# Two transformer-like blocks on one core: the projections beside the scan as pairs of 2x2 block products, and the scan's input and results kept in DRAM

## The reference

```python
h = rmsnorm(x, norm_pre)
proj = h @ w_in
xbc, dt_raw, z_ssd, sc_h, sc_b, sc_c, z_sc = jnp.split(proj, idx, axis=-1)
xbc = silu(causal_dwconv(xbc, ssd_conv_w, ssd_conv_b))      # 10 tiles of 128
y_ssd = ssd_chunked(xs, dt, a, bm, cm, d_skip)              # the scan, 8 chunks of 128 tokens
yz = y_ssd * silu(z_ssd);  y_ssd = rmsnorm(yz)              # 8 tiles
v = causal_dwconv(sc_c * sc_h, sc_conv_w)                   # 8 + 8 tiles
y_sc = sc_b * v * silu(z_sc)                                # 8 + 8 tiles
x = x + rmsnorm(concat(y_ssd, y_sc) @ w_out, norm_post)     # then a gate; then block two
```

## Time and profile before

| | |
|---|---|
| runs | 2523.59, 2518.59, 2519.59 us |
| median | 2519.59 us |
| profiled execution | 2521.91 us |
| its span, first to last instruction | 2520.2 us |
| mean granted TensorE clock | 0.986 |
| DMA queues, mean over the span | 97 GB/s |

### The profile page before, as it was taken

One profiled execution on the slowest core, in us unless ns is written; L12 is line 12 of the kernel. 1 busy time (PEld: TensorE's weight loads), 2 busy tenths in 40 slices (PEclk: granted clock), 3 DMA queues, 4 the chain that ended last, 5 costly groups with the idle time before them and its releaser, 6 DMA issues.

```text
span 2520.2 us, 34207 instructions
## 1 busy us (share of the span) xinstructions
PE 2424.8 (96%) x12962; PEld 1985.4 (79%) x12962; DVE 1479.8 (59%) x1930; ACT 738.6 (29%) x946; POOL 1053.4 (42%) x561
## 2 busy tenths in 40 slices
PE   7999999999999899999999999999989999899995
PEld 5777888887888678777878787788877888788885
DVE  6766556556621462113156766745788666777788
ACT  4332232222200221242022222222264333343443
POOL 4433333334443554233223223233464555466661
PEclk9999999999999999999999999999999999999998
DMA  5122122213111332122222222222224444843321
GB/s 203 42 68 75 58 87 72 75 62 113 34 50 50 100 101 77 42 98 85 75 80 77 78 63 83 70 87 84 66 102 150 151 168 142 312 185 139 123 101 67
DMA packets 100937, 245.62 MB, mean 97 GB/s; under 512 B 10850, under 2 KB 36706, under 8 KB 96243
## 3 DMA queue, kind: packets, MB, share of 16 engines
q1 hardware_dynamic: 59904, 186.67, 22.2%
q10 hardware_dynamic: 40946, 57.78, 6.7%
HBM read 183.53 MB, written 60.88 MB: 97 GB/s over the span
## 4 chain that ended last, share of the span: by engine, by line
PE 80%; DVE 10%; issue 4%; ACT 2%; DMA 2%; POOL 2%; ACTq 0%; DVEq 0%; SPq 0%; POOLq 0%
PE pt L2020 47%; PE pt L2413 14%; PE wk L2413 6%; PE pt L2036 1%; PE pt L2050 1%; DMA eb<-o_d 1%; PE wk L2319 1%; PE wk L2424 1%; PE wk L2175 1%; PE wk L2289 1%; PE wk L2354 1%; DVE eb L1684 1%; PE wk L2353 1%; PE wk L2075 1%; PE wk L2176 1%
## 5 line engine op out<-in xcount | busy, mean ns | idle before, releaser
L545 POOL TENSOR_TENSOR w_hi<-w_raw,ones 128x1024 fp32r<-128x1024 f32 x138 | 269.4, 1953 | 1109.5 <-PE pt L2020 1056.5
L549 POOL TENSOR_TENSOR w_lo<-w_raw,w_hi 128x1024 fp32r<-128x1024 f32 x138 | 381.8, 2766 | 10.9
L2020 PE MATMUL pt<-xh,w_hi 128*128 128x512 f32 x960 | 300.3, 394 | 2.4 <-ACT ea L791 2.4
L2020 PE MATMUL pt<-xh,w_lo 128*128 128x512 f32 x960 | 296.6, 390 | 0.0
L2020 PE MATMUL pt<-h,w_hi 128*128 128x512 f32 x896 | 290.9, 406 | 1.8 <-ACT cu_o L903 1.8
L2020 PE MATMUL pt<-l,w_hi 128*128 128x512 f32 x896 | 278.0, 391 | 0.0
L2020 PE MATMUL pt<-h,w_lo 128*128 128x512 f32 x896 | 277.2, 391 | 0.0
L2020 PE MATMUL pt<-xl,w_hi 128*128 128x512 f32 x848 | 263.0, 391 | 0.0
L2020 PEld LDWEIGHTS pt<-xh,w_hi 128*128 128x128 f32 x960 | 179.5, 189 | 47.0 <-issue 9.4
L2020 PEld LDWEIGHTS pt<-xh,w_lo 128*128 128x128 f32 x960 | 181.0, 189 | 38.1
L2020 PEld LDWEIGHTS pt<-l,w_hi 128*128 128x128 f32 x896 | 168.8, 188 | 36.6
(11 more groups left out here) (520 smaller groups left out, 5066.5 us busy)
## 6 DMA issues: line engine op xcount, KB each, us to landing
w_raw<-ws_d SPq DMA_DIRECT2D x140, 512.0 KB, 3.6
fx_d<-stg SPq DMA_DIRECT2D x106, 256.0 KB, 2.6
fraw<-ws_d SPq DMA_DIRECT2D x32, 512.0 KB, 5.0
raw<-ws_d SPq DMA_DIRECT2D x32, 512.0 KB, 8.3
xs0f<-fx_d SPq DMA_DIRECT2D x10, 1024.0 KB, 4.8
xs1f<-fx_d SPq DMA_DIRECT2D x9, 1024.0 KB, 4.9
xs2f<-fx_d SPq DMA_DIRECT2D x9, 1024.0 KB, 5.0
x_raw<-xT_d SPq DMA_DIRECT2D x32, 256.0 KB, 7.2
```

What stands on the lines that cost most here:

```text
L545: nc.gpsimd.tensor_tensor(out=w_hi[:, u, :], in0=w_raw[:, u, :], in1=zeros, op=ALU.add).then_inc(w_hi_done, 1)
L549: nc.gpsimd.tensor_tensor(out=w_lo[:, u, :], in0=w_raw[:, u, :], in1=w_hi[:, u, :].bitcast(f32), op=ALU.subtract).then_inc(w_split, 1)
L2020: ins = MM(pt[:, slot, h * HALF:(h + 1) * HALF], wt[:, k * P:(k + 1) * P], x[:, k, h * HALF:(h + 1) * HALF], start=first and k == 0 and n ...
```

## The change

The 32 tiles beside the scan become 16 pairs. A pair's weights are four blocks of 512 inputs by 128 outputs, x is four blocks of 512 features by 512 tokens, and the pair's result (2 x 128 features by 2 x 512 tokens) is made of seven block products in place of eight, each 4 row blocks x 3 matmuls. The products need sums of weight blocks (two on DVE, two on POOL per pair) and differences of x blocks, which replace x in `x_raw` once (16 subtractions on DVE, high halves `thi` by ACT, low halves `tlo` by POOL, between the first and second convolution pair). `tlo` takes the place of `xbc`, `thi` that of `vbuf`. So the scan's input goes to DRAM (`xbc_d`) and each chunk is loaded from there by SP; the chunk's result goes to `ys_d`, the branch to `sv_d`, and both are loaded again after the scan. One block of x, `xh` and `xl` rows 0 to 3 of the second token half, isn't needed beside the scan: it is stored in `x12_d`, its place holds the ring of four weight slots, and it is loaded again for the tiles `S_SB`.

```diff
+SC_PAIRS = 2 * C
+SC_ORDER = (1, 6, 7, 5, 4, 2, 3)
@@ SyncE
+        weights(1, 4, 0)
+        sp.wait_ge(stat_done, 2)
+        sc_load(0)
...
+        for j in range(C):
+            n = 2 * j
+            if j < C - 1:
+                sp.wait_ge(sw_lo, 7 * n + 7)
+                sc_load(n + 2)
+            sp.wait_ge(y_evac, j + 1)
+            sp.dma_start(ys_d.rearrange("i p t -> p i t")[:, :, j * P:(j + 1) * P], yb[:]).then_inc(ys_put, 16)
+            if j < C - 1:
+                chunk_load(j + 1)
...
+        for n, x in enumerate((xh, xl)):
+            sp.dma_start(x[:, 0:4, cols(1)].bitcast(f32), x12_d[n, :, :, :]).then_inc(x12_in, 16)
...
+        for i in range(5, KT):
+            y_load(i)
+            v_load(i - 3)
@@ GpSimd
-        for u in range(2):
-            split(u, 16)
-            rest(u, u + 1)
+        split(0, 16)
+        rest(0, 1)
+        rest(1, 2)
...
+        for j in range(1, S_SB // 2):
+            for u in range(2):
+                pool.wait_ge(mm_done, j * 2 + u - 1)
+                split(u, j * 16 + 16)
+                rest(u, j * 2 + u + 1)
+            if j > 1:
+                for i in range(4 * j - 8, 4 * j - 4):
+                    difference_lo(i)
...
+        for g in range(SC_PRODUCTS):
+            n, i = divmod(g, 7)
+            sc_lo(g)
+            if i == 5:
+                fourth_sum(n)
+                if n < SC_PAIRS - 1:
+                    third_sum(n + 1)
@@ ScalarE
         xbc_pair(0)
...
+        for i in range(16):
+            r, c = difference(i)
+            act.wait_ge(xt_done, i + 1)
+            A(thi[:, r, c], x_raw[:, r, c], ACT.Copy).then_inc(xth_done, 1)
         xbc_pair(1)
...
+            A(sc_slot(g)[0], sc_factor(n, p), ACT.Copy).then_inc(sw_hi, 1)
...
+            tanh(j, 1)
+            if not last:
+                sc_hi(b + 8)
+                if j:
+                    decay_rows(j + 1, 0, 8)
+            sc_11(2 * j + 1)
+            tanh(j, 2)
+            if not last:
+                sc_hi(b + 9)
+                if j:
+                    decay_rows(j + 1, 8, HEADS)
...
+            tanh(j, 3)
...
         def branch_high(i):
-            act.wait_ge(mm_done, S_SB + i + 1)
+            act.wait_ge(mm_done, S_SB + max(i + 1, 2))
@@ VectorE
         conv_pair(0)
+        for k in range(4):
+            for m in range(4):
...
+                if m:
+                    dve.wait_ge(xt_done, 4 * k + m)
+                TT(out=x_raw[:, r, c], in0=x, in1=y, op=ALU.subtract).then_inc(xt_done, 1)
         conv_pair(1)
...
+        def part_x(n):
...
+            TT(out=sx5[:], in0=bank(3), in1=su2[:], op=ALU.add).then_inc(sc_part, 1)
...
+        for j in range(C):
+            a, b = 2 * j, 2 * j + 1
+            part_u2(a)
+            weight_sums(b)
+            if j > 1:
+                scan_input(j)
+            part_x(a)
+            if j > 1:
+                scan_decayed(j)
+            part_22(a)
...
+            tap(j, 1)
+            part_u2(b)
+            tap(j, 2)
+            if j < C - 1:
+                weight_sums(b + 1)
+            if j == 0:
+                scan_matrix(j)
+            elif j > 1:
+                scan_out(j)
+            part_x(b)
+            if j == 1:
+                scan_out(j)
+            if j:
+                scan_state(j)
+            part_22(b)
+            if j:
+                gate_z(j, 1)
+            part_21(b)
...
+            gate_z(j, 0)
...
+            gate_branch(j, 0)
...
+            part_12(b)
+            gate_branch(j, 1)
@@ TensorE
-        pe.wait_ge(p_lo_done, 2)
...
-            for k in range(2):
-                for m, (wt, x) in enumerate(((w_hi, p_hi), (w_hi, p_lo), (w_lo, p_hi))):
+            for m, (wt, x) in enumerate(((w_hi, p_hi), (w_lo, p_hi), (w_hi, p_lo))):
...
+        def sc_product(g):
...
+            out = bank((0, 1, 3, 2, 3, 0, 2)[i])
+            pe.wait_ge(sw_lo, g + 1)
...
+            elif i == 0:
+                pe.wait_ge(sc_t1, 2 * n)
+                if n > 1:
+                    pe.wait_ge(sc_th, (n // 2 - 1) * 4 + 3)
+            elif i < 4:
+                pe.wait_ge(sc_part, 5 * (n - 1) + (1, 4, 5)[i - 1])
+            elif i == 5:
+                pe.wait_ge(sc_t1, 2 * n + 1)
+            else:
+                pe.wait_ge(sc_part, 5 * n + (2 if i == 4 else 3))
+            w = sc_slot(g)
+            for k in range(4):
+                x = sc_operand(p, k)
+                for m, (wt, xx) in enumerate(((w[0], x[0]), (w[0], x[1]), (w[1], x[0]))):
+                    ins = MM(out, wt[:, k * P:(k + 1) * P], xx, start=i < 4 and k == 0 and m == 0, stop=k == 3 and m == 2, skip_group_check=True)
+            ins.then_inc(sc_prod, 1)
...
+        for j in range(C):
+            for i in range(14):
+                sc_product(14 * j + i)
+                if i == (5 if j == 0 else 3 if j == 1 else 1):
+                    scan_first(j)
+                if i == (11 if j == 0 else 9 if j == 1 else 8):
+                    scan_second(j)
```

More of the change, by code:

```diff
@@ L586, in _ @@
+        pool.wait_ge(v_done, 3 * C)
+        for u in range(2):
+            split(u, 16 * (S_SB // 2 + 2))
+            rest(u, S_SB + 3 + u)
+        split_pairs(S_SB // 2 + 2, S_GATE // 2)
         before_norm(S_GATE)
@@ new lines, in sc_11, with tanh @@
+        def sc_11(n):
+            act.wait_ge(sc_prod, 7 * n + 6)
+            act.wait_ge(sc_part, 5 * n + 1)
+            A(st1[:], bank(0), ACT.Copy).then_inc(sc_t1, 1)
+        def tanh(j, m):
+            n = 2 * j + 1
+            if m == 2:
+                act.wait_ge(sz_done, 2 * j + 1)
+            else:
+                act.wait_ge(sc_part, 5 * n + (3, 4, 0, 5)[m])
+                if m == 3:
+                    act.wait_ge(sz_done, 2 * j + 2)
+                elif j:
+                    act.wait_ge(v_done, 3 * j)
+            A(th[:, m % 2, :], (s22[:], sx5[:], bank(0), su2[:])[m], ACT.Tanh, scale=0.5).then_inc(sc_th, 1)
@@ new lines, in first_tap @@
+        def first_tap(j):
+            act.wait_ge(u_done, 2 * j + 2)
+            if j:
+                act.wait_ge(sv_put, 16 * j)
+            A(vj[:], ecp[:, 0:T], ACT.Identity, scale=V("sc_w", j)).then_inc(tap_done, 1)
+        act.wait_ge(x12_free, 1)
+        act.wait_ge(x12_put, 32)
+        for g in range(3):
+            sc_hi(g)
+        xbc_copy(XBC_T // 2 - 1, 0)
+        sc_hi(3)
+        xbc_copy(XBC_T // 2 - 1, 1)
+        xbc_silu(XBC_T // 2 - 1, 0)
+        for j in range(C):
+            a, b = 14 * j, 14 * j + 7
+            last = j == C - 1
+            if j:
+                sc_hi(a + 3)
+            sc_first(2 * j)
+            if j > 1:
+                decay_exp(j)
+            sc_hi(a + 4)
+            sc_hi(a + 5)
+            if j == 0:
+                xbc_silu(XBC_T // 2 - 1, 1)
+            elif j == 1:
+                in_decay(j)
+            else:
+                state_rows(j)
+            sc_hi(a + 6)
+            if j == 1:
+                decay_rows(j, 0, 8)
+                state_rows(j)
+            sc_hi(a + 7)
+            if j == 0:
+                act.wait_ge(xbc_put, 16 * XBC_T)
+                rows_load(0)
+            elif j == 1:
+                decay_rows(j, 8, HEADS)
+                decay_exp(j)
+            sc_hi(a + 8)
+            sc_11(2 * j)
+            if j == 0:
+                act.wait_ge(adt_done, 1)
+                in_decay(j)
+                state_rows(j)
+            sc_hi(a + 9)
+            if j == 0:
+                decay_rows(j, 0, 8)
+            sc_hi(b + 3)
+            sc_first(2 * j + 1)
+            if j == 0:
+                decay_rows(j, 8, HEADS)
+            first_tap(j)
+            if j == 0:
+                decay_exp(j)
+            sc_hi(b + 4)
+            sc_hi(b + 5)
+            if j and not last:
+                rows_load(j + 1)
+            sc_hi(b + 6)
+            tanh(j, 0)
+            if not last:
+                sc_hi(b + 7)
+                if j:
+                    in_decay(j + 1)
+            tanh(j, 1)
+            if not last:
+                sc_hi(b + 8)
+                if j:
+                    decay_rows(j + 1, 0, 8)
+            sc_11(2 * j + 1)
+            tanh(j, 2)
+            if not last:
+                sc_hi(b + 9)
+                if j:
+                    decay_rows(j + 1, 8, HEADS)
+                else:
+                    rows_load(j + 1)
+            tanh(j, 3)
@@ new lines, in part_21, with part_12, scan_input @@
+        def part_21(n):
+            dve.wait_ge(sc_prod, 7 * n + 5)
+            dve.wait_ge(sc_part, 5 * n + 3)
+            TT(out=sx5[:], in0=bank(3), in1=su2[:], op=ALU.add).then_inc(sc_part, 1)
+        def part_12(n):
+            dve.wait_ge(sc_prod, 7 * n + 7)
+            dve.wait_ge(sc_part, 5 * n + 4)
+            TT(out=su2[:], in0=bank(2), in1=su2[:], op=ALU.add).then_inc(sc_part, 1)
+        def scan_input(j):
+            dve.wait_ge(ssd_a, j + 1)
+            if j:
+                dve.wait_ge(ys_put, 16 * j)
```

(9 more changed lines are left out.)

512 lines of the change are left out of this document (374 added, 138 removed).

## The result

The changed kernel takes 2534.68 us (median of 2533.39, 2534.49, 2534.86 and 2538.70); beside it the kernel before takes 2520.41. The ratio is 1.0052, 95% interval 1.0035 to 1.0068: **slower by 0.5%**, where the forecast was 1% faster. The profiled execution has 2538.7 us, a span of 2536.5 and a mean clock of 0.975 (0.986 before, with a span of 2520.2).

What follows compares the result with a forecast made beforehand. The prediction took TensorE's own work as the bound; products -40, differences +18.2, tail -1.1 and start -3 sum to -25.9 us, so 2519.6 becomes 2493.7 us, range 2473 to 2513.

Steps and rivals of the forecast that it cites:

- Part 1, the products: Scan stage: 84 matmuls per pair of tiles instead of 96, stage 365 us against 405.0, -40 us.
- The wait per chunk: Scan, from the third chunk on: TensorE waits 0.7 us per chunk for the next first product's bank, bounds 0 and 2.5.
- The first chunk: Scan start: product 5 waits 0.7 us for `part_x(0)`, and `part_x(1)` is ready about 2.9 us after product 11 ends.
- The clock: Scan stage: no loss to lower clock counted behind the waits.
- rival (b): Scan: each chunk's wait brings 2.2 us of lower clock, or waits are 2.5 us; 2508 us, chance 0.18.
- the feed-forward row at 0.99: Feed-forward stage: already runs the seven products with the same ring at clock 0.99; cited against lower clock in the scan.
- rival (c): Scan: DVE, held by POOL, becomes the bound at 50.6 us a chunk; slower, 2537 us, chance 0.10.
- half of the holds: Scan: POOL holds DVE for nothing to 18 us per chunk; 9 us taken, DVE at 42 of 44.5 us.
- Part 2, the differences: Before the scan: 16 DVE subtractions in turns with POOL leave TensorE idle 16 us, 2.2 for clock; +18.2 us, bounds 0 and 20.
- Part 3, the tail: From last scan product to the sums: `v_done` sooner, 2.3 us given back at `branch_high(0)`; -1.1 us, bounds -6 and +6.
- Part 4, the start: Kernel start: TensorE no longer waits for `p_lo`, ACT makes the second high half; -3 us, bounds -1.5 and -5.
- Rival (a): Before the scan: the differences are hidden, 0 to 4 us in place of 18.2; 2478 us, chance 0.20.

Runs made afterwards that it cites:

- c_rows_between: Changed kernel with ScalarE's two next-chunk exponentials ahead of the first tanh and eight decay rows between first and second tanh: 2517.76 us, 0.9982 of the kernel before.
- c_chunk0: Changed kernel with, in the first chunk only, DVE's releasing additions ahead of weight sums and scan matrix, ScalarE's first tap earlier: 2528.22 us, 1.0012 of the kernel before.
- comb3: Changed kernel with differences spread, XBC high halves on ScalarE, c_rows_between, t_all, extended c_chunk0, DVE's gate chain overlapped, y loads earlier: 2488.05 us, 0.9855 of the kernel before.
- x_lows_late: Changed kernel with only GpSimd's eight low halves of the x differences moved behind later weight splits: 2536.1 us, a single run.
- t_all: Changed kernel, tail only: last branch tile kept in SBUF, weights and first gate tile loaded earlier, first two evacuations earlier: 2527.57 us, 1.0014 of the kernel before.

## Why the prediction was wrong

**Part 1, the products.** Right in its core: 44.5 us a chunk was forecast; `c_rows_between` does its last six in 270.2 us (284.7 to 554.9), 45.0 each, at a clock of 1.00, where the forecast with its wait had 45.2. Wrong in what stands around it, 31.4 us of 40, in three pieces.

- *The wait per chunk, 0.7 us forecast, 2.4 measured* (bounds 0 and 2.5). DVE's `part_21` came where forecast. The failing step is the walk on ACT: "They stand behind `tanh(j, 1)` (which follows DVE's `part_21` ...)". Two exponentials of 1.06 us stand ahead of that tanh, and the eight decay rows took 2.43 us, not 1.3 to 2.2. 6 x 0.7 was 4.2, measured 14.8. `c_rows_between` shows it: those two moved, the waits are gone.
- *The first chunk, 3.6 us forecast, 11.2 measured.* The places were right, `part_x(0)` and `part_x(1)`, the sizes not: DVE's weight sums and scan matrix ahead of `part_x(1)` took 7.6 us with their holds (1.64, 1.63 and 4.48) and were reckoned nearly free of them, and ahead of them the tap waited until 212.2 for ACT, behind 2.43 us of decay rows. `c_chunk0` shows the order to be the cause: the stage is 9.1 us shorter.
- *The clock, 0 forecast, 11.9 of the remaining 13.6 us.* That is rival (b), which asked for waits of 2.5 us or for lower clock behind the waits, 13 to 18 us: both happened, the lower clock behind four of the six waits and in the first chunk. The forecast held the feed-forward row at 0.99 against it. The ring of four banks is indeed not the cause, since with the waits gone it runs at 1.00 (284.7 to 554.9 in `c_rows_between`); the waits were. (The Trainium skill, TensorE: Matmul & The Clock Gate, "A second HAM failure mode: psum-queue depth-cycling", ties the loss to small idle times between groups while banks are cycled; of the two, the runs here bear out the idle times.) `c_rows_between` keeps 3.9 us of lower clock, all in the first chunk. The last 1.7 us (some 4 in `comb3`, of 370.5 - 356.2 - 6.5 = 7.8) are short gaps and were not isolated.

**DVE as the bound**, rival (c), did not happen in the scan: in `c_rows_between` DVE is busy for 37 us of a chunk (70.58 x 45.0 / 85), where 42 were taken, ACT for 21 where 24 were. So half of the holds was too many on average and too few in the first chunk, where they stood on the path. The forecast put none on POOL's side: it is busy for 31 us of a chunk (59.46 x 45.0 / 85) where 23.2 were reckoned, since POOL waits for its turn too.

**Part 2, the differences.** Mechanism and place right, size near: idle 12.5 against 16, clock 2.4 against 2.2. `x_lows_late` shows the turns. What the forecast did not see is that the stage has hardly a free place for them: spread out, they cost TensorE 8.5 us in this stage instead of 12.5.

**Part 3, the tail: -1.1 forecast, +10.6 measured, outside the bounds of -6 and +6.** The failing step is "45 us, as long as the chain that they feed": it put the transfer and the chain side by side as averages. What counted were single transfers at the chain's head: the first gate tile (5.8 us in front of everything), the weights behind 2 MB of x (their splits ended at 602.3, due at 597.3), a buffer that waits for its own store. Bandwidth was better than reckoned, 398 to 417 GB/s and not 316. `v_done` also came 7 us after the last product and not 3.2: two instructions of DVE were held to 2.38 and 2.77 us by POOL's splits. `t_all` and `comb3` show the repair.

**Part 4, the start.** -1.2 against -3, outside the bound of -1.5. The gain that was forecast is there at first: TensorE reaches its first sums at 22.3 us instead of 25.2. From there to the XBC pairs it takes 20.7 us instead of 19.0, and the granted clock says why (windows of before, then of after, with this stretch in them):

```profile
25.00:44.00 19.00, 16.28 (x76) 12.82 (x76) 15.56 (x31) 12.31 (x18) 5.32 (x3) 1.00 0.39 142
```

```profile
22.00:43.00 21.00, 17.84 (x76) 13.99 (x76) 15.98 (x32) 12.45 (x18) 6.43 (x5) 0.92 0.50 186
```

Behind a wait of 2.1 us at the sums the clock falls for a time, (1 - 0.92) x 21 = 1.7 us lost; the kernel before waits there for 1.0 us and keeps 1.00. The term that failed is again the clock behind a wait, put at nothing. Twelve of the thirteen profiled kernels with the new start show a lowering in this stretch; they begin their XBC pairs at 42.4 to 44.4 us, and the one without it at 41.9.

Rival (a) is excluded by `x_lows_late`. The slower outcome came by none of the rivals alone. Rival (b) reckoned 14 us over the forecast; it took the scan's 31.4 and the tail's 11.7 (10.6 + 1.1) together.

## What to carry to other kernels

An engine with half its time free can still set the pace: walk its list entry by entry up to the instruction that frees the bank, with everything for the *next* iteration that stands ahead of it. Price a short wait of TensorE above its length where it returns every iteration: 13.2 us of waits removed here gave 14 to 19, since the granted clock fell behind two to four of the six waits in each execution. For data sent through DRAM, ask for each consumer when its first tile is asked for, what its buffer waits for and what is ahead on the queue; the sum of bytes over a bandwidth says nothing about the head of the chain.
